# Two expert mixtures inside a hybrid layer stack: one more weight chunk is fetched ahead of the routing, and the last two expert pairs are run together

## What is computed

```python
def hier_moe(x, w_group, w_expert, w_gate, w_up, w_down):
    g_prob = softmax(xf @ w_group); g_sel = argmax(g_prob)              # 4 groups
    top_p, top_i = top_k(softmax(e_logits[g_sel]), 2)                   # 2 of the group's 8 experts
    ...
    def expert_block(args):
        xb, e = args
        h = silu(xb @ w_gate[e]) * (xb @ w_up[e])                       # 1024 -> 512
        return h @ w_down[e]                                            # 512 -> 1024
    ...
h = layer_norm(DEEPNORM_ALPHA * h + mix, ln_mix_g[layer], ln_mix_b[layer])
ffn = hier_moe(h, ...)
h = layer_norm(DEEPNORM_ALPHA * h + ffn, ln_ffn_g[layer], ln_ffn_b[layer])
```

## Time and profile before

| | |
|---|---|
| median of 3 runs | 1813.28 us (1812.97 to 1813.47) |
| the profiled execution | 1812.31 us, of which the trace spans 1810.5 us |
| granted TensorE clock | 1.00, full, over the whole span |
| PE busy | 1760.7 us, 97% of the span |
| DVE, ACT, POOL busy | 36%, 25%, 4% |
| moved by DMA | 527.35 MB, mean 291 GB/s |
| the chain that ended last | 79% PE, 18% DMA, 2% DVE, 1% ACT |

### The profile page before, as it was taken

The page is one execution under the profiler, slowest core; times in us unless marked ns, Lnnn a source line. Parts: engine busy times, 40 slices in busy tenths (PEclk is TensorE's granted clock), DMA queues, the critical chain, the costliest instruction groups (busy, mean ns, idle before and its releaser), DMA issues.

```text
span 1810.5 us, 20279 instructions
## 1 busy us (share of the span) xinstructions
PE 1760.7 (97%) x8218; PEld 989.1 (55%) x8223; DVE 655.8 (36%) x1569; ACT 444.3 (25%) x956; POOL 70.9 (4%) x66
## 2 busy tenths in 40 slices
PE   9999999999988899999999999889999999999999
PEld 8888754444434333455444434333366767568874
DVE  3566753111111112035321111011245566344675
ACT  2332311111110100134111111010135534217780
POOL 0000000000000000000000000000011110001110
PEclk9999999999999999999999999999999999999999
DMA  9723569999999999708899999999942323041520
GB/s 387 305 85 136 197 257 381 428 428 427 428 428 428 427 428 416 318 1 339 333 430 428 428 428 427 428 427 428 417 186 93 140 115 118 6 181 47 235 91 24
DMA packets 41536, 527.35 MB, mean 291 GB/s; under 512 B 4768, under 2 KB 5440, under 8 KB 8544
## 3 DMA queue, kind: packets, MB, share of 16 engines
q1 hardware_dynamic: 39200, 518.80, 68.9%
q10 hardware_dynamic: 2240, 7.21, 1.0%
HBM read 524.91 MB, written 1.08 MB: 291 GB/s over the span
## 4 chain that ended last, share of the span: by engine, by line
PE 79%; DMA 18%; DVE 2%; ACT 1%; issue 0%; POOL 0%; DVEq 0%; ACTq 0%
PE ps L220 32%; PE ps L871 16%; DMA ring<-in_wu 15%; PE ps L903 9%; PE ps L714 2%; DMA ring<-in_wg 2%; PE ps L808 2%; PE ps L920 2%; PE ps L1694 2%; PE ps L1662 2%; PE ps L1226 1%; PE ps L678 1%; PE ps L1709 1%; PE ps L1438 1%; PE ps L1451 1%; PE ps L878 1%
## 5 line engine op out<-in xcount | busy, mean ns | idle before, releaser
L871 PE MATMUL ps<-ring,work 128*64 128x512 f32 x1856 | 414.5, 595 | 35.9 <-DMA ring<-in_wu 22.7
L871 PEld LDWEIGHTS ps<-ring,work 128*64 128x64 f32 x1856 | 131.4, 137 | 306.7 <-issue 249.8
L220 PE MATMUL ps<-xl,ring 128*128 128x256 f32 (+3 forms) x1344 | 291.4, 375 | 0.0
L220 PEld LDWEIGHTS ps<-xl,ring 128*128 128x128 f32 x1344 | 243.7, 190 | 38.9 <-issue 2.5
L903 PE MATMUL ps<-ring,work 128*64 128x512 f32 x832 | 185.6, 596 | 0.5 <-ACT work L1893 0.4
L2625 DVE TENSOR_TENSOR work<-work,ps 128x512 f32<-128x512 f32 x32 | 22.0, 687 | 443.1 <-PE ps L871 376.7
L220 PE MATMUL ps<-ring,xl 128*128 128x256 f32 (+1 forms) x576 | 176.0, 463 | 0.2 <-ACT xl L1779 0.2
L220 PEld LDWEIGHTS ps<-ring,xl 128*128 128x128 f32 x576 | 108.3, 190 | 59.3 <-issue 49.9
L903 PEld LDWEIGHTS ps<-ring,work 128*64 128x64 f32 x832 | 57.4, 137 | 101.9 <-issue 99.7
L3153 POOL TENSOR_TENSOR small<-small,halves 128x1 f32<-128x1 f32 (+4 forms) x42 | 45.7, 1087 | 1550.1 <-DVE small L2436 941.8
L2590 DVE SCALAR_TENSOR_TENSOR yr<-ps,small,yr 128x512 fp32r<-128x512 f32 x60 | 45.0, 750 | 162.9 <-ACT yr L1908 162.9
(11 more groups left out here) (461 smaller groups left out, 1861.8 us busy)
## 6 DMA issues: line engine op xcount, KB each, us to landing
ring<-in_wg SPq DMA_DIRECT2D x62, 2048.0 KB, 28.1
ring<-in_wu SPq DMA_DIRECT2D x52, 2048.0 KB, 30.3
ring<-in_wd SPq DMA_DIRECT2D x50, 2048.0 KB, 29.9
xl<-in_wd SPq DMA_DIRECT2D x10, 2048.0 KB, 34.0
xl<-in_wu SPq DMA_DIRECT2D x9, 2048.0 KB, 25.7
ring<-in_w_odd SPq DMA_DIRECT2D x8, 2048.0 KB, 8.1
ring<-in_w_xz SPq DMA_DIRECT2D x7, 2048.0 KB, 22.5
ring<-in_w_qkv SPq DMA_DIRECT2D x6, 2048.0 KB, 22.1
```

The costliest lines, as they stand in the source:

```text
L220: i = e.matmul(bout, lhs(k), rhs(k), start=start and k == ks[0], stop=stop and k == ks[-1])
L871: last = e.matmul(b[64 * j:64 * j + 64, :], x[:, 4 * a + k, 64 * j:64 * j + 64], w[k // 2][:, 2 * (k % 2) + j, :], start=a + k == 0, stop= ...
```

## The change

1. **One chunk more aside.** `ASIDE` gets ("mu", 0, 1). The chunk ("mg", 0, 1), and after it ("md", 0, 1), now lies whole in `big`; ("mu", 0, 1) goes to new places `beside`: the part of `work` (after the router's logits) and `lnb`, the parameters of the layer norm (after that norm). The parameters of the second norm go to `lnf`, in `big`. `xl` now takes ("mg", 1, 1), earlier in the queue of layer 0. So eleven chunks are issued before the first gate matmul.
2. **Queue of SP.** `MOE_CHUNKS` sets the order. Chunks ("md", 1, 0) and ("md", 1, 1) are now issued ahead of the asides; the issue of ("mg", 2, 0) takes the freed slot that ("md", 1, 1) had.
3. **The last two pairs.** Gate and up of pairs 14 and 15 come first, then the four down chunks, all in halves (`HALVED`), the last half in quarters. PE's list follows: `tensor_down` of pair 14 stands behind the turning of pair 15. The turned rows of pair 15 get a place of their own (`hT15`), since `hT` is still read. ACT and DVE move the rows of pair 14 behind the hidden rows of pair 15.
4. **Small moves.** ACT casts `h` to `hr` behind pair 0 and no longer ahead of it. `load_ln` waits for `gat_mm` of pair 15 in place of `spr_mm` of pair 14. In layer 1 the slot of qkv (1, 2) is given out one place later. Scratch of the norms (`zjunk`) and of the branch for crowded experts moves.

The core of the diff:

```diff
-TAIL = (15, 1)
-PARTED, EARLY = ("mu", 2, 1), ("mu", 0, 1, 0)
-ASIDE = [("mg", 0, 1), ("md", 0, 1)]
+HALVED = ((14, 0), (14, 1), (15, 0), (15, 1))
+PARTED, EARLY = ("mu", 2, 1), ("mg", 0, 1, 1)
+ASIDE = [("mg", 0, 1), ("md", 0, 1), ("mu", 0, 1)]
...
+        MOE_CHUNKS = [(name, p, a) for p in range(NE // 2 - 2) for name in ("mg", "mu", "md") for a in range(2)] + [
+            (name, p, a) for names in (("mg", "mu"), ("md",)) for p in (NE // 2 - 2, NE // 2 - 1) for name in names
+            for a in range(2)]
...
-            ring.order.insert(6, ring.order.pop())
+            ring.order.insert(6 if l else 4, ring.order.pop())
...
-        aside = [big[:, 2048:4096], xgT[:, 1].rearrange("p k n -> p (k n)")]
+        aside = [big[:, 0:2048], big[:, 2048:4096]]
+        beside = [xgT[:, 1].rearrange("p k n -> p (k n)"), lnb[:, :, :].rearrange("p a n -> p (a n)")]
...
+        lnf = area(big, 1024, (2, 1024))
...
-                    if p == NE // 2 - 1:
-                        tensor_spread(e, l, p - 1, ((0, 0), (0, 1)))
...
+            hx_ = hT15 if p == NE // 2 - 1 else hT
+            for n in ns:
...
-                if (p, n) == TAIL:
-                    landed = {0: (tail_in, 16 * (l + 2)), 3: landed[0]}
+                if (p, n) in HALVED:
+                    landed = {0: (half_in[p, n][0], half_in[p, n][1] + 16 * (l + 1)), 2: landed[0]}
+                if (p, n) == HALVED[-1]:
+                    landed[2], landed[3] = (quarter_in, 16 * (l + 2)), landed[2]
...
                     tensor_turn_h(e, l, p)
                     tensor_spread(e, l, p - 1, SUMS[2:4])
                     tensor_slots(e, l, p + 1)
-                    tensor_down(e, l, p)
                 else:
-                    tensor_spread(e, l, p - 1, SUMS[2:3])
                     tensor_turn_h(e, l, p)
-                    tensor_spread(e, l, p - 1, SUMS[3:4])
+                    tensor_down(e, l, p - 1)
+                    tensor_spread(e, l, p - 1, SUMS[0:2])
                     v = e.value_load(flag(l))
-                    tensor_down(e, l, p)
+                    tensor_down(e, l, p, (0,))
+                    tensor_spread(e, l, p - 1, SUMS[2:4])
+                    tensor_down(e, l, p, (1,))
...
         def scalar_moe(e, l):
-            e.wait_ge(*ln_out(f"m{l}", 1, 1))
-            e.copy(hr[:, 0], h[:, 0:2, :]).then_inc(*high_in.up(l))
...
+                if p == 0:
+                    e.copy(hr[:, 0], h[:, 0:2, :]).then_inc(*high_in.up(l))
...
+                        if (name, p, a) == ("mg", 2, 0):
+                            if l:
+                                sync_aside(e, A["wg"][l, 0, 1], ao_mm(1, 1, 1), (0,))
+                            else:
+                                sync_aside(e, A["wg"][l, 0, 1], out_mm("p4"))
+                            sync_aside(e, A["wu"][l, 0, 1], lg_mm(l, 1), (0,), beside, beside_in)
...
+                            sync_aside(e, A["wu"][l, 0, 1], ln_out(f"m{l}", 1, 1), (1,), beside, beside_in)
+                        if (name, p, a) == ("mg", 2, 1):
                             sync_aside(e, A["wd"][l, 0, 1], gate_mm(l, 0, 1))
...
-            e.wait_ge(*spr_mm(l, NE // 2 - 2))
+            e.wait_ge(*gat_mm(l, NE // 2 - 1, 1))
             load_ln(e, 2 * l + 1)
```

More of the change, by code:

```diff
@@ L410, in build @@
             ring.last(x)
+        late_v = ring.order.pop(ring.order.index(ring.chunks["qkv", 1, 2][0]))
+        ring.order.insert(ring.order.index(ring.chunks["qkv", 1, 1][0]) + 1, late_v)
         ring_moe(1)
@@ L515, in build @@
         zdiag = [area(work, 6656 + t * 128, (128,)) for t in range(2)]
-        zjunk = [area(big, 1024 + i * 512, (512,)) for i in range(4)]
+        zjunk = [area(big, 3072, (512,)), area(big, 3584, (512,)), lnb[:, 1, 0:512], lnb[:, 1, 512:1024]]
         m = Arena(work, 7680)
@@ L860, in tensor_hidden @@
                         w = [kview(4, 512)(v) for v in aside]
+                    elif (name, p, a) == ASIDE[2]:
+                        e.wait_ge(beside_in, 32 * l + 32)
+                        w = [kview(4, 512)(v) for v in beside]
                     else:
@@ L1879, in scalar_gathered, with scalar_rows_high @@
                    ).then_inc(*xg1.up(l, s))
+        def scalar_rows_high(e, l, p):
+            e.wait_ge(*swt_in(l, p))
+            if p:
+                e.wait_ge(*spr_mm(l, p - 1))
+            for n in range(2):
+                e.wait_ge(*dn_mm(l, p, n))
+                e.activation(yr[:, 0, n * 512:(n + 1) * 512], row_b[n][:, :], ACT.Copy, scale=wsl[:, p % 2:p % 2 + 1]
+                             ).then_inc(*yh.up(l, p, n))
         def scalar_moe(e, l):
-            e.wait_ge(*ln_out(f"m{l}", 1, 1))
-            e.copy(hr[:, 0], h[:, 0:2, :]).then_inc(*high_in.up(l))
             scalar_gathered(e, l, 0)
@@ L3214, in sync_part, with sync_aside @@
             e.dma_start(ring.view(*key)[:, c], w[:, c]).then_inc(landed, 16)
-        def sync_aside(e, w, gone, halves=(0, 1)):
+        def sync_aside(e, w, gone, halves=(0, 1), place=aside, landed=aside_in):
             e.wait_ge(*gone)
             for half in halves:
-                e.dma_start(aside[half], w[:, 2048 * half:2048 * half + 2048]).then_inc(aside_in, 16)
+                e.dma_start(place[half], w[:, 2048 * half:2048 * half + 2048]).then_inc(landed, 16)
         def sync_moe(e, l):
-            for p in P16:
-                for name, w in (("mg", A["wg"]), ("mu", A["wu"]), ("md", A["wd"])):
-                    for a in range(2):
-                        if (name, p, a) in ASIDE:
-                            continue
-                        if (name, p, a) == (("mu", 1, 1) if l else ("md", 1, 1)):
-                            sync_aside(e, A["wg"][l, 0, 1], sc_mm(7, 1) if l else out_mm("p4"), (0,))
-                        if (name, p, a) == ("md", 1, 1):
-                            sync_aside(e, A["wg"][l, 0, 1], lg_mm(l, 1), (1,))
+            weights = {"mg": A["wg"], "mu": A["wu"], "md": A["wd"]}
+            for name, p, a in MOE_CHUNKS:
+                    if (name, p, a) not in ASIDE:
+                        w = weights[name]
+                        if (name, p, a) == ("md", 1, 0) and l:
+                            sync_aside(e, A["wg"][l, 0, 1], sc_mm(7, 1), (1,))
+                        if (name, p, a) == ("mg", 2, 0):
+                            if l:
+                                sync_aside(e, A["wg"][l, 0, 1], ao_mm(1, 1, 1), (0,))
+                            else:
+                                sync_aside(e, A["wg"][l, 0, 1], out_mm("p4"))
+                            sync_aside(e, A["wu"][l, 0, 1], lg_mm(l, 1), (0,), beside, beside_in)
```

72 lines of the change are left out of this document (40 added, 32 removed).

## The result

The changed kernel is slower by 0.3%: 1819.93 us median against 1812.87 for the kernel of before on the same chip, ratio 1.0031 with a 95% interval of 1.0022 to 1.0039. I had forecast 1810.6, with a range of 1808.2 to 1813.5. The executions of the changed kernel lie apart, from 1812.38 to 1822.51 us, most of them near 1818 or 1822; those of before lie within 1812.15 to 1815.07. Since they lie so far apart, their median says little by itself: the two medians alone would give 1.0039, the upper end of the interval. The profiled execution took 1822.46 us (span 1820.7).

What follows compares the result with a forecast made beforehand. PE bounds each mixture's first half and weight landings at 427 GB/s the rest; 1.8 us from mixture 0 plus 0.9 from mixture 1 gives 2.7 us, so 1810.6 us median, range 1808.2 to 1813.5.

Steps and rivals of the forecast that it cites:

- Other code ahead of it may move that pause away: Rival: the 1.28 us idle behind the flag's branch in mixture 0 goes; 4.0 us gained in all, 1809.3; chance 0.09.
- the starved queue: Slower rival: loads run dry three times between 294.4 and 308.2, each restart costing 1.5 us more; 1819.6 us; chance 0.05.
- The lead: Start of each mixture: an eleventh chunk issued before the first gate matmul leaves 0.9 us of its 4.94 us.
- The spare of 0.9 us: Loads behind the start: least margin, at the seventeenth chunk, ready to flow at 308.2 against the data's arrival at 309.1.
- Nothing is left of the lead and the end: Rival: short stops eat the 0.9 us and the load of the register is long; 1813 us; chance 0.10.
- The end of mixture 0: Last pairs: PE, no longer the last landing, ends it at 708.2, 0.9 us sooner; 1.8 us with the lead's 0.9.
- The end of mixture 1: Behind the mixture PE waits for the landing of `lat`, so only 0.9 us of the 1.8 is gained.
- The sum: Whole kernel: 1.8 us from mixture 0 and 0.9 from mixture 1, 2.7 us faster.
- The five loads more in each mixture: Four from cutting the last four chunks finer, one from the aside in two halves; costed at nothing.
- The fixed part: 2.0 us for each DMA; if paid in turn, the ten added loads cost 20 us, 1831; chance 1 in 100.

Runs made afterwards that it cites:

- the one with its loads held back: Changed kernel with the load of LN's parameters and every chunk behind it on SP's queue waiting for pair 15's last down chunk; 1822.30 us.
- the waits in mixture 0: 100 idle, long-fulfilled PE waits, ten ahead of each of pairs 4 to 13 in mixture 0: kernel of before 1810.70 us, changed kernel 1811.30 us.
- the tail alone: Kernel of before with 100 idle waits in mixture 0, the change's order of the last two pairs and its place for LN's parameters, old lead; 1810.06 us.
- the two tails: New order of the last pairs on the old lead, 100 idle waits in mixture 0: LN's parameters at the old place 1811.56 us, at the new 1810.06.

## Why the prediction was wrong

**The step that failed** is one that I had as a rival and not as a term: "Other code ahead of it may move that pause away". I gave the pause behind the branch one direction, "goes", and a price of at most its 1.28 us. It can as well grow, to 4.71 us, come up where none was (mixture 1), and bring the clock down behind it for 1.6 or 1.7 us more. The forecast's own sum has no term for it. Together this is 2.0 + 1.6 + 4.7 + 1.7 = 10.0 us of the 10.2 of the profiled execution. It was not in reach of my slower rival, the starved queue at 1819.6 us, either: the time is near, the cause another. I had the row of 1.28 us in the earlier trace rows and asked what it would be worth if it went, not on what it hangs. Of the changed kernel and the 15 versions tried, the four whose branch was held for over 6 us have medians of 1819.9 to 1822.3, and the eleven others, without the one with its loads held back, lie below 1815.

**The lead**, 0.9 us in each mixture, was mis-sized: it is no gain, and in mixture 0 it costs. In the changed kernel the last up chunk of pair 14 starts at 667.80, less 0.6 of late start 667.2, against 666.85; with the waits in mixture 0 it is 667.01 against 666.11, from the same start. Over all traces the time from the first gate product to this chunk is 391.5 to 392.6 us with the old lead (nine, mean 391.95) and 392.3 to 393.2 with the new (eight, mean 392.77): 0.8 us more. The mechanism was the one that I described, and SP's issue of ("mu", 2, 0) is at 297.01, as before but for the start:

```profile
285.48 0.33 SPq L3240 DMA_DIRECT2D ring<-in_wg  x1
297.01 0.33 SPq L3240 DMA_DIRECT2D ring<-in_wu  x1
302.17 2.04 SPq L3243 DMA_DIRECT2D ring<-in_wu  x2
```

The stretches of the changed kernel have the price (last numbers DMA share, GB/s):

```profile
295.00:300.00 5.00, 5.00 (x26) 1.72 (x24) 0.75 (x1) 0.69 (x1) 0.00 (x0) 1.00 0.42 131
300.00:305.00 5.00, 5.00 (x26) 1.62 (x24) 2.79 (x2) 2.47 (x2) 0.00 (x0) 1.00 0.95 387
305.00:310.00 5.00, 5.00 (x26) 1.68 (x24) 0.26 (x1) 0.60 (x1) 0.00 (x0) 1.00 1.00 356
```

From 280 to 320 us 14.52 MB move, and 16.79 in before: 2.27 MB less, 5.3 us at 427 GB/s, against the 4.9 us of the chunk that was ahead. The spare of 0.9 us was worked out as if the line of data ran at 427 up to each stop and at once behind it; around each stop it runs thinner (131, 387 and 356 GB/s here, 433, 408 and 401 before), and that eats 1.2 to 1.8 us. This is the first case of my rival *Nothing is left of the lead and the end*, for the lead alone.

**The end of mixture 0**, 0.9 us shorter on PE, was right in its steps: my sum from the last up chunk of pair 14 to the last sums was 41.35 us, and 41.32 were measured; `swt` is waited for (0.99 us), and PE and not the last quarter ends it. **The end of mixture 1** was right in its bound: with the pauses out of the way `lat` is what PE waits for, 0.98 us in the changed kernel with the waits and 0.94 in the tail alone. Not foreseen was how much of the tail's worth hangs on a load that I costed at nothing, LN's parameters: 1.4 to 1.5 us between the two tails.

**The sum** without the pauses would be: changed kernel 1811.30 against 1810.70 for before, both with waits, so 0.6 us slower where my sum has 2.7 faster. That is within 0.1% and the executions overlap (1810.88 to 1812.18 against 1810.00 to 1811.33), so what is shown is that the 2.7 us aren't there. Both begin the last sums of mixture 0 at 708.32, since the tail's 0.9 pays for the lead's; and as `lat` follows the line of data, the product with its second half starts at 1305.68 against 1304.47, 1.2 us late at the end.

The five loads more in each mixture, costed at nothing, cost nothing that shows: with the halves and quarters in the queue 410 to 444 GB/s moved from 696 to 712 us. The fixed part that the prediction weighs for them, from the Trainium skill, "DMA: Bandwidth & Descriptors", stands in that page's section "Anatomy of one DMA — SWDGE (gpsimd) path" and is for loads issued by GpSimd; these are issued by SP.

**Left open:** why some executions of the changed kernel take 1812.4 us. Their mean granted clock is 1.000, as that of the one with 1814.24, where the nine slower ones have 0.997 or 0.998; so the clock didn't fall in them, which fits with pauses that were short or absent. A block's load that comes in time there would explain it, but there is no profile of such an execution. Open too is when PE asks for a block: the trace shows only the packet.

## What to carry to other kernels

An idle row behind a branch with no releaser was here the loading of instructions, and is a reason to look for the instruction packets beside it; before an edit ahead of such a branch is judged, find where the edges stand against the branch, its target and the sequencer's long waits ahead of it, and time the edit also with idle instructions added, in more than one number. Put those where the engine waits for data anyway, since in a part that is bound by the engine they cost what they take. An additional one-time buffer ahead of a ring that is full when the stream begins only brought the stop forward here: compare the bytes moved in the stretch behind, not the lead at its start.

## What the runs showed of the hardware

- With the data queue full, the packet of a block of PE's instructions started 3.6 to 4.2 us behind the start of the branch, in all nine pauses of that kind. With the queue nearly empty it started 1.3 us ahead of the branch in one mixture, which had no pause, and 0.9 behind it in the other. Where there was a pause, PE went on 2.2 to 2.9 us after the packet's start.
- Where the branch itself was held for over 6 us, the packet started 6.2 to 6.4 us after the end of the sequencer's wait ahead of it (four cases).
- PE's branch took 6.16 to 6.29 us in one mixture of four kernels, 3.65 in one, and 0.24 to 0.82 us in all others.
- Behind pauses of 1.28, 1.49 and 2.08 us the sums ran at full clock (3.70 us for eight); behind each of 3.22 us and more they ran in part at the lower level, 4.4 to 5.3 us for six and 5.4 to 6.7 for eight. A wait for weights or for DVE was followed by a fall too, in each of the five cases of 2.56 to 2.84 us (two of them in the run with the late loads), and in none of the five of 2.00 to 2.40.
- 100 to 221 instructions more on PE, waits that were long fulfilled, cost 1.7 to 2.5 us in the scan and nothing that shows in the mixture.
